# Seven block products for five units a layer, the column units one stage later, and a new order in two later stages

## The chip, the core and the metric

The kernel runs on one NeuronCore of a Trainium2 chip. The metric is the device time of one execution in microseconds (us), the median of several runs. TensorE is called PE here, VectorE DVE, ScalarE ACT, GpSimd POOL, and SyncE, which only issues transfers, SP.

## The reference

The input is one sequence of 256 tokens by 1024 features, in float32. It passes through two blocks; each has two layers.

```python
def first_block(x, ...):
    for l in range(2):
        u = rms_norm(x, pre_norm_g[l]) @ w_in[l]        # 1024 -> latent, sb, moba, conv, gate columns
        o_a = mla_attention(...)                         # from 352 latent columns and two up matrices
        o_b = stick_breaking_attention(q_b, k_b, v_b)    # 4 heads of 64
        o_c = moba_attention(q_c, k_c, v_c, rel_bias)    # 4 heads of 64, biased by distance
        o_d = conformer_conv(u_conv, ...)                # 31 taps, layer norm, 256x256
        y = concat(o_a, o_b, o_c, o_d) * silu(u_gate)    # 1024 gate columns
        x = x + rms_norm(y @ w_out[l], post_norm_g[l])

def second_block(x, c, w_ada, ...):
    for i in range(2):
        sh1, sc1, g1, sh2, sc2, g2 = split(silu(c) @ w_ada[i] + b_ada[i], 6)
        u = x * (1 + sc1) + sh1
        y = gla_mixer(u) if i == 0 else chunk_attention(u)     # 16 heads of 64 in the attention
        x = layer_norm(alpha * x + (1 + g1) * y)
        u = x * (1 + sc2) + sh2
        y = square(relu(u @ ff_w1[i])) @ ff_w2[i]              # 1024 -> 4096 -> 1024
        x = layer_norm(alpha * x + (1 + g2) * y)
```

The row c has 1024 features and is the same for all tokens, so silu(c) @ w_ada is a product of a vector and a matrix: 2 layers of 1024x6144.

## The kernel before

The stages follow each other on one core: first block, layer 0 and layer 1; the input product of the GLA mixer, its chunks and its output; feed-forward 0; the attention in four groups of four heads ("qd" 0 to 3 in the code); feed-forward 1. Each engine has one program of its own, written out by hand, and waits on semaphores; nothing is planned at run time. An instruction never passes another on the same engine, so the order of the calls in each engine's block is the order of the work.

**Weights.** All large weights are cut into units of 128x2048 float32 (1 MB). They lie in one array in the order of use, and SP (L483) copies unit n into slot n modulo 6 of the tile `raw` as soon as unit n-6 has been used. SP issues strictly in order: unit n+1 isn't issued before unit n. The orders are strings: in the first block, "w" is a weight unit and "a" a column unit; in the mixer "m" and "a"; in a feed-forward "u" (up), "d" (down) and "a".

**Column units.** The 48 units of w_ada are multiplied by the row silu(c) on DVE: column_unit (L982) runs two multiply-and-reduce instructions over 128x1024 for one unit, which then frees its slot. Before, 12 of them stand in each layer of the first block, 11 in the GLA mixer and 13 in feed-forward 0. `coefficients(s)` (L1062 and on, a few small instructions) turns their sums into the scale and shift of stage s.

**A layer of the first block.** unit_t (L1971) multiplies one unit by the transposed tokens hT: 16 matmuls of 128 weight columns by 256 tokens, which the profile counts as 32 (a float32 matmul has two records), and which give 256 columns of the product. Ten units go through it in a layer: U_CA, U_CG, U_BQ, U_BK, U_CQ, U_CK and four gate units; the value units have a form of their own (L1981), the latent units go through first_units (L2024). The order on PE is: latent products; conv, stick-breaking and moba units; the scores; for each pair of heads a gate unit, the transposes of the probabilities (turn, L1998), the product with the values (L2164), and in between the conv's transposes (L2219, which need cnat from DVE L1315) and its 256x256 product (L2234, into a bank that gate 3 has to be read out of first); then the output product in seven block products (L2040). On DVE the order is: norms, column units, the conv's 31 taps, the stick-breaking sums (L1232 to L1244), then per pair: gate (L1256), two score maxima (head_max, L1046 and L1049), their reciprocals (L1056), one column unit; after the second pair the conv's mean and variance (L1305), inv_root (L964 to L973) and cnat.

**Seven block products.** For output products, GLA inputs, feed-forwards and attention projections the kernel already uses a scheme of Strassen's kind: a 2x2 block product by seven block products in place of eight, with sums of weight blocks and of token blocks before and sums of products after. The sums are on DVE (mixer_weights L1725 to L1730, mixer_sums L1738 and on, up_sums L1590 to L1595), in the attention on POOL (quad_weights L578 to L583, four instructions for one unit) and DVE (quad_sums L1864 to L1873).

**The attention.** Its 16 units are W0 to W15, in that order with nothing between. For qd = 0, 1, 2 POOL runs quad_weights(3*qd+3), then head_biases(qd+1) (L593 to L596: the value bias and the table of distances of the next four heads), then quad_weights of the two units after it; quad_weights(u) works on the unit W(3+u). DVE runs two maxima, quad_sums(3*qd), two maxima, the next queries (L1885), reciprocals 2 and 3 (L1056), quad_sums(3*qd+1), in the first two groups two pieces of the residual (L1544), quad_sums(3*qd+2), the group's output (L1943) and the next group's value rows (L1894, which wait for head_biases). PE runs the seven products of the units (quad_unit, L2625) between the scores, the turns and the products with the values.

**Feed-forward.** In a group g, PE runs half of the up products of group g+1 (L2342), the first half of the down products of group g (L2315), the rest of the up products, and the second half of the down products.

```python
with sp.Fori(1, N_UNITS // SLOTS) as i:                                         # L480
    for s in range(SLOTS):
        sp.wait_ge(used[s], i)
        sp.dma_start(raw[:, s, :], units[i * SLOTS + s, :, :]).then_inc(landed[s], 16)
```

Of the kernel before, what the change touches and what calls it, by code (L numbers as in the profile page):

```python
# [11 lines left out]
ALU = mybir.AluOpType  # L12
ACT = mybir.ActivationFunctionType
# [24 lines left out]
A1 = 12  # L38
# [5 lines left out]
ORDER = "wwwawwawwawawawa" "wawawawa" "wwawwa"  # L44
# [5 lines left out]
U_GATE = (U_G0, U_G1, U_G2, U_G3)  # L50

# [30 lines left out]
GLA_ORDER = 4 * "mma" + "mmaaaa" + "mmmmmmaaa"  # L82
FF_ORDER = ("u" + 13 * "uda" + "ud" + "dud", "u" + 14 * "ud" + "dud")
# [3 lines left out]
N_FF1 = N_ATT + 16  # L87
# [10 lines left out]
AG = len(GA_AT)  # L98

ADA_1 = [N_GLA + n for n in GA_AT] + places(FF_ORDER[0], "a", N_FF0)  # L100
assert len(GW_AT) == 16 and len(ADA_1) == 24
# [34 lines left out]
def build(nc, x, units, cols, small, post_g, consts, onehot, rel_bias, crow_in, colb_in,  # L136
          ln_rows, low_in, gk_in, att_line, v_row, out):
    with ExitStack() as ctx:  # L138
# [13 lines left out]
        HB = ((G[2], G[3]), (G[0], G[1]))  # L152
# [114 lines left out]
        early = sb("early", [P, 4, P])  # L267
# [52 lines left out]
        ones_ready, rr_psum, rr_ready = sem("ones_ready"), sem("rr_psum"), sem("rr_ready")  # L320
# [17 lines left out]
        qk_ready = event("qk_ready", 4)  # L338
# [23 lines left out]

        fixed_ready = sem("fixed_ready")
        colb_ready, gla_in, lnrow_in, line2_in = (sem(n) for n in ("colb_ready", "gla_in", "lnrow_in", "line2_in"))
        gcol_ready, gate_out, row_in = sem("gcol_ready"), sem("gate_out"), [sem(f"row_in{g}") for g in range(2 * DEPTH)]
        tb_ready = sem("tb_ready")
# [68 lines left out]
        OUT_UNITS.append(tuple(N_ATT + 12 + w for w in range(4)))  # L435
# [7 lines left out]
        OUT_W.append([[ada[:], xs[:, 1, :], row(tline), crow[:]],  # L443
# [8 lines left out]
        out_block = [gateT[:].rearrange("p a b -> p (a b)")[:, 512 * i:512 * (i + 1)] for i in range(4)]  # L452

# [36 lines left out]
        def _(pool):  # L490
# [5 lines left out]
            pool.memset(relb[:], 1.0).then_inc(ones_ready, 1)  # L496
# [24 lines left out]
            pool.wait_ge(ones_ready, 1)  # L521
# [26 lines left out]
            store_gate(0)  # L548
            for l in range(1, DEPTH):
                layer_vectors(l)  # L550
            store_gate(1)

            pool.wait_ge(x_new.sem, 2 * DEPTH + 2)
            for g in range(2):
                load_gate(g)
# [7 lines left out]

            norm_rows(1)
# [4 lines left out]
            def quad_weights(u):  # L569

                n = N_ATT + 3 + u
# [4 lines left out]
                if u >= 3:  # L576
                    wait_used(pool, 0, n - 3)
# [13 lines left out]
            def head_biases(qd):  # L591
                pool.wait_ge(line2_in, 16 * (qd + 2))
                pool.tensor_copy(vcur[:], vrow[:, GW * qd:GW * (qd + 1)]).then_inc(cur_ready.sem, 1)  # L593
                pool.tensor_copy(tcur[:], tline[:, :, ::-1]).then_inc(tb_ready, 1)
                pool.wait_ge(tb_ready, qd + 1)
# [9 lines left out]

            store_gate(3)
            load_gate(3)
# [17 lines left out]
            norm_rows(2)  # L625
            norm_rows(3)

        @block.scalar
        def _(act):
# [79 lines left out]
            for l in range(DEPTH):  # L709
# [54 lines left out]
                wait_used(act, T1 * l, U_CQ)  # L764
                act.activation(qkC[:, 0], G[0][:], ACT.Copy, scale=HD_SCALE).then_inc(qk_ready.sem, 1)
                wait_used(act, T1 * l, U_CK)
                act.activation(qkC[:, 1], G[1][:], ACT.Copy).then_inc(qk_ready.sem, 1)
# [7 lines left out]

                def gate_tanhs(g):
                    wait_used(act, T1 * l, U_GATE[g])
                    if g >= 1:
                        act.wait_ge(silu_ready.sem, silu_ready.at(l, g))
                    act.activation(th[:].rearrange("p c s -> p (c s)"), G[1][:], ACT.Tanh, scale=0.5).then_inc(gate_tanh.sem, 1)  # L780
# [7 lines left out]
                for g in range(H):  # L788
                    gate_tanhs(g)
                    for j in (2 * g, 2 * g + 1):  # L790
                        head_copy(8 * l, j, (A[3], A[0]))
                    if g < H - 1:
# [118 lines left out]
            def keys(qd):  # L911
                act.wait_ge(bc_ready.sem, bc_ready.at(qd, 1))
                if qd == 0:
                    wait_used(act, 0, N_ATT + 1)
# [42 lines left out]
        def _(dve):  # L957
# [31 lines left out]
            def gate_columns(g, n):  # L989

                wait_used(dve, 0, n)
                dve.wait_ge(colb_ready, 16)
                dve.scalar_tensor_tensor(gcol[:, g, :], gacc[:, g, :], 1.0, colb[:, B_GATE + KC * g:B_GATE + KC * (g + 1)],
                                         ALU.add, ALU.add).then_inc(gcol_ready, 1)
# [1903 lines left out]
```

## Time and profile before

| | us |
|---|---|
| median of 3 runs (lowest, highest) | 976.6 (975.53, 977.18) |
| the profiled execution, whole | 975.87 |
| its span, first to last instruction | 974.0 |
| PE busy | 957.1 |
| DVE busy | 758.5 |
| ACT busy | 230.7 |
| POOL busy | 83.7 |

| stage, us from the span's start | PE busy | DVE busy | POOL busy | DMA share |
|---|---|---|---|---|
| layer 0, 0 to 155.4 | 153.5 | 110.5 | 11.5 | 0.68 |
| layer 1, 155.4 to 304 | 146.8 | 111.7 | 4.3 | 0.58 |
| GLA mixer, 304 to 432 | 127.6 | 115.2 | 2.5 | 0.61 |
| feed-forward 0, 432 to 640 | 206.0 | 187.3 | 7.9 | 0.71 |
| attention, 640 to 760 | 119.9 | 73.6 | 56.9 | 0.44 |
| feed-forward 1 and the end, 760 to 974 | 203.3 | 160.2 | 0.5 | 0.39 |

A row of the timeline gives the start, the time to the end, the engine, the line, the operation with its output and input, the shape (partitions on both sides for a matmul, then partitions by columns) and the number of like instructions merged. In square brackets stands the idle time just before it and what ended it; a row without brackets started with no idle time worth showing. The end of a matmul is modelled and overlaps the next one, so the pitch of matmuls is read from start to start.

### The profile page before, as it was taken

How to read it: one execution, taken by the hardware profiler on the slowest of the kernel's cores; microseconds unless marked ns; L12 is line 12 of the kernel's file. 1: busy time of each engine (PE TensorE's matmuls, PEld its weight loads, DVE VectorE, ACT ScalarE, POOL GpSimd, SP SyncE). 2: the span in 40 equal slices, each digit the busy share in tenths (PEclk: the TensorE clock that was granted, in tenths of full speed). 3: DMA queues.
4: the chain of work that ended last, by engine and by line, in shares of the span. 5: the costliest groups of instructions: out<-in, count | busy, mean ns of one | idle time of the engine just before them, and what ended most of it. 6: DMA issues, size and time to landing. Idle time of an engine off the chain costs nothing. (4 is left out here: it accounts for less than half of the span.)

```text
span 974.0 us, 14339 instructions
## 1 busy us (share of the span) xinstructions
PE 957.1 (98%) x5354; PEld 711.0 (73%) x5354; DVE 758.5 (78%) x1719; ACT 230.7 (24%) x580; POOL 83.7 (9%) x100
## 2 busy tenths in 40 slices
PE   9999999999999999999999999999999999999996
PEld 5858855858857998757777777689994767777764
DVE  2796687696688898999999888955667877766687
ACT  4134425125433222111000000123333200000002
POOL 2100000000001000000001000056830000000000
PEclk9999999999999999999999999999999999999999
DMA  9954653855555766574779777535444254544411
GB/s 354 379 201 191 234 201 149 350 197 226 196 215 209 288 220 257 178 297 149 245 289 336 284 257 259 189 131 195 152 173 147 103 184 173 216 173 174 173 44 44
DMA packets 31069, 205.38 MB, mean 211 GB/s; under 512 B 3640, under 2 KB 4845, under 8 KB 7709
## 3 DMA queue, kind: packets, MB, share of 16 engines
q1 hardware_dynamic: 27740, 190.94, 52.9%
q0 software_dynamic: 3264, 13.57, 3.9%
q8 instruction: 43, 0.70, 0.3%
q14 instruction: 22, 0.17, 0.1%
HBM read 203.42 MB, written 1.07 MB: 210 GB/s over the span
## 5 line engine op out<-in xcount | busy, mean ns | idle before, releaser
L1971 PE MATMUL bank<-hT,raw 128*128 128x256 f32 x736 | 162.5, 380 | 0.0
L1971 PEld LDWEIGHTS bank<-hT,raw 128*128 128x128 f32 x736 | 138.9, 190 | 21.2 <-issue 2.4
L982 DVE CUSTOM_DVE_ANT_0 raw<-raw,crow 128x1024 f32<-128x1024 f32 x96 | 113.2, 1222 | 6.7 <-DMA raw<-units_dram 5.3
L2315 PE MATMUL bank<-yT,arena 128*128 128x512 f32 x224 | 100.8, 593 | 0.1
L2315 PE MATMUL bank<-raw,arena 128*128 128x512 f32 x180 | 86.8, 593 | 0.0
L2315 PEld LDWEIGHTS bank<-yT,arena 128*128 128x128 f32 x224 | 42.5, 190 | 54.0 <-issue 51.9
L2342 PEld LDWEIGHTS bank<-hT,raw 128*128 128x128 f32 x416 | 50.4, 192 | 11.5 <-issue 11.5
L839 ACT ACTIVATE arena<-bank 128x512 f32<-128x512 f32 x26 | 15.6, 598 | 179.3 <-PE bank L2342 179.3
L2342 PE MATMUL bank<-hT,raw 128*128 128x128 f32 x416 | 50.6, 275 | 0.0
L1024 DVE SCALAR_TENSOR_TENSOR arena<-arena 128x256 f32<-128x256 f32 x120 | 49.2, 485 | 0.1
L2342 PE MATMUL bank<-arena 128*128 128x128 f32 x336 | 42.2, 275 | 3.0 <-issue 3.0
L2342 PEld LDWEIGHTS bank<-arena 128*128 128x128 f32 x336 | 39.8, 192 | 4.6 <-issue 4.6
L2342 PE MATMUL bank<-arena,gateT 128*128 128x128 f32 x336 | 42.1, 275 | 0.0
L2315 PEld LDWEIGHTS bank<-raw,arena 128*128 128x128 f32 x180 | 29.9, 191 | 16.3 <-issue 16.3
L2342 PEld LDWEIGHTS bank<-arena,gateT 128*128 128x128 f32 x336 | 39.8, 192 | 0.0
L2040 PE MATMUL bank<-arena 128*128 128x512 f32 x88 | 39.7, 592 | 0.0
L2342 PEld LDWEIGHTS bank<-arena,raw 128*128 128x128 f32 x224 | 29.4, 192 | 13.4 <-issue 13.4
L841 ACT ACTIVATE arena<-bank 128x384 f32<-128x384 f32 x28 | 13.8, 492 | 106.8 <-PE bank L2342 106.8
L2286 PE MATMUL bank<-hT,raw 128*128 128x128 f32 x244 | 37.4, 283 | 1.3 <-ACT hT L700 1.1
L2286 PEld LDWEIGHTS bank<-hT,raw 128*128 128x128 f32 x244 | 33.0, 191 | 4.3 <-issue 3.0
L1602 DVE TENSOR_TENSOR arena<-arena 128x256 f32<-128x256 f32 x26 | 11.4, 440 | 31.0 <-ACT arena L839 30.8
L2040 PEld LDWEIGHTS bank<-arena 128*128 128x128 f32 x88 | 16.6, 190 | 19.8 <-issue 19.7
(471 smaller groups left out, 1767.9 us busy)
## 6 DMA issues: line engine op xcount, KB each, us to landing
raw<-units_dram SPq DMA_DIRECT2D x178, 1024.0 KB, 4.9
arena<-ln_rows_dram POOLq DMA_DIRECT2D x4, 1024.0 KB, 5.0
arena<-gate_scratch POOLq DMA_DIRECT2D x4, 512.0 KB, 5.5
arena<-att_line_dram POOLq DMA_DIRECT2D x4, 512.0 KB, 5.8
arena<-small_dram POOLq DMA_DIRECT2D x2, 896.0 KB, 10.5
raw<-units_dram SPq DMA_DIRECT2D x2, 704.0 KB, 7.5
xt<-x_dram SPq DMA_DIRECT2D x2, 512.0 KB, 5.4
arena<-post_g_dram POOLq DMA_DIRECT2D x2, 512.0 KB, 8.4
```

What stands on the lines that cost most here:

```text
L839: act.activation(prod[:, 0:4].rearrange("p i n -> p (i n)"), A[0][:], ACT.Copy).then_inc(prod_ready.sem, 1)
L841: act.activation(prod[:, 4:7].rearrange("p i n -> p (i n)"), A[0][:, 0:3 * P], ACT.Copy).then_inc(prod_ready.sem, 1)
L982: ins = dve.tensor_tensor_reduce(out=w, in0=w, in1=crow[:], scale=1.0, scalar=0.0, op0=ALU.mult, op1=ALU.add, accum_out=dst[:, c:c + 1])
L1024: ins = dve.scalar_tensor_tensor(cacc[:, c, :], xg[:, c, j:j + S], w, cacc[:, c, :], ALU.mult, ALU.add)
L1602: ch.do(dve.tensor_tensor(csum[:, 0:5:4], p[:, 0:1].to_broadcast([P, 2, P]), p[:, 1:3], ALU.add))
L1971: mm = pe.matmul(b[:, c * S:(c + 1) * S], raw[:, s, k * 256 + c * P:k * 256 + (c + 1) * P], act_t[:, k, :], start=(k == 0), stop=(k == KC ...
L2040: mm = pe.matmul(OUT_BANKS[l][j][:], x[c] if isinstance(x, list) else x[:, c], y[c] if isinstance(y, list) else y[:, 512 * c:512 * (c + 1) ...
L2286: mm = pe.matmul(b[:, c * S + t * P:c * S + (t + 1) * P], raw[:, n % SLOTS, k * 256 + c * P:k * 256 + (c + 1) * P], hT[:, k, t * P:(t + 1) ...
L2315: mm = pe.matmul(SB[i][:], x, y, start=g == 0, stop=stop)
L2342: mm = pe.matmul(b[:, i * P:(i + 1) * P], x(k), y(k), start=k == 0, stop=k == 3)
```

## The change

Five units of each layer of the first block, U_CQ, U_CK and gates 1 to 3, are multiplied by seven block products: first_tokens makes four sums of token blocks once a layer, first_weights four instructions of 128x512 for a unit (one writes into the unit itself), first_seven 28 matmuls of 128 columns by 128 tokens (56 records in the profile), ACT two copies out of the banks, first_outputs six instructions of 128x128 and 128x256. Gates 1 to 3 are read from the tile `early` in place of a bank. Gate(g) now stands on DVE after first_outputs, the two maxima and the reciprocals of its pair; before, it stood ahead of them.

The 48 column units keep their number and their own cost, but 6 stand in each layer of the first block, 12 in the mixer, 12 in feed-forward 0, 8 in the attention and 4 in feed-forward 1. coefficients(1) stands in the middle of the mixer in place of its start.

In both feed-forwards the products of group 1 get another order; POOL's loading of two gate rows is moved; at the seam of the layers ACT does the second layer's first tile in two halves; in the GLA input the second tile's transposes come two steps earlier.

```diff
-ORDER = "wwwawwawwawawawa" "wawawawa" "wwawwa"
+ORDER = "wwwawwa" "wwwawwa" "wwawwa" "wwww"
-GLA_ORDER = 4 * "mma" + "mmaaaa" + "mmmmmmaaa"
-FF_ORDER = ("u" + 13 * "uda" + "ud" + "dud", "u" + 14 * "ud" + "dud")
+GLA_ORDER = 4 * "mma" + "mmaaaa" + "mmmmmmaaaa"
+ATT_ORDER = "www" "aa" "wwwa" "aa" "wwwa" "aa" "wwwwwww"
+FF_ORDER = ("u" + 2 * "ud" + "aua" + 10 * "dua" + "du" + "ddud",
+            "u" + 2 * "ud" + "aua" + 2 * "dua" + 9 * "du" + "ddud")
+ATT_UNITS = ((0, 1), (2, 3, 4), (5, 6, 7), ())
@@ ACT, first block
+                for i, (u, b) in enumerate(((U_CQ, G[0]), (U_CK, A[2]))):
+                    act.activation(first_prod[i][:, 0:4]..., b[:], ACT.Copy, scale=scale)
+                    wait_used(act, T1 * l, u)
+                    act.activation(first_prod[i][:, 4:7]..., G[1][:, 0:3 * P], ACT.Copy, scale=scale)
@@ ACT, seam of the layers
                     y_square(l, 1, 0)
+                    layer_input(l + 1, 0, 0, KC // 2)
                     y_square(l, 1, 1)
-                    layer_input(l + 1, 0, 0, KC)
+                    layer_input(l + 1, 0, KC // 2, KC)
@@ DVE, first block
+            def first_tokens(l):
+                ch.do(dve.tensor_tensor(first_tsum[:, 0], b[0][1], b[0][0], ALU.subtract))
+                ch.do(dve.tensor_tensor(first_tsum[:, 2], b[1][1], b[0][1], ALU.subtract))
+                ch.do(dve.tensor_tensor(first_tsum[:, 1], b[1][1], first_tsum[:, 0], ALU.subtract))
+                dve.tensor_tensor(first_tsum[:, 3], b[1][0], first_tsum[:, 1], ALU.subtract)
+            def first_weights(l, i):
+                wait_landed(dve, T1 * l, U_SEVEN[i])
+                ch.do(dve.tensor_tensor(d[1], a[0][0], a[1][0], ALU.subtract))
+                ch.do(dve.tensor_tensor(a[1][0], a[1][0], a[1][1], ALU.add))
+                ch.do(dve.tensor_tensor(d[0], a[1][0], a[0][0], ALU.subtract))
+                dve.tensor_tensor(d[2], a[0][1], d[0], ALU.subtract)
+            def first_outputs(l, i, o):
+                dve.wait_ge(fprod_ready.sem, fprod_ready.at(l, 2 * i + 2))
+                ch.do(dve.tensor_tensor(c[:, 0], p[:, 0], p[:, 2], ALU.add))
+                ch.do(dve.tensor_tensor(o[:, 0], p[:, 0], p[:, 1], ALU.add))
+                ch.do(dve.tensor_tensor(c[:, 1], c[:, 0], p[:, 3], ALU.add))
+                ch.do(dve.tensor_tensor(c[:, 2], c[:, 0], p[:, 5], ALU.add))
+                ch.do(dve.tensor_tensor(o[:, 2:4], c[:, 1:2]..., p[:, 4:6], ALU.add))
+                ch.do(dve.tensor_tensor(o[:, 1], c[:, 2], p[:, 6], ALU.add))
+                first_tokens(l)
                 if l == 0:
                     silu_row()
-                    ada_unit(l, 0)
-                ada_unit(l, 1)
+                    ada_unit(0)
+                ada_unit(A1 * l + 1)
...
-                ada_unit(l, 2)
+                ada_unit(A1 * l + 2)
                 taps(0, 12)
-                ada_unit(l, 3)
                 taps(12, 20)
...
+                first_weights(l, 0)
+                first_weights(l, 1)
                 taps(20, TAPS)
-                ada_unit(l, 4)
...
-                ada_unit(l, 5)
-                ada_unit(l, 6)
+                first_outputs(l, 0, qkC[:, 0]...)
+                ada_unit(A1 * l + 3)
...
+                first_outputs(l, 1, qkC[:, 1]...)
+                first_weights(l, 2)                        # ahead of the loop over the heads
                 for j in range(2 * H):
                     if j % 2 == 0:
-                        gate(j // 2)
+                        if j == 0:
+                            gate(0)
+                        else:
+                            first_outputs(l, 1 + j // 2, early)
...
-                        if j < 6:
-                            ada_unit(l, 7 + j // 2)
+                        if j > 0:
+                            gate(j // 2)
+                        if j == 2:
+                            first_weights(l, 4)
+                        if j < 4:
+                            ada_unit(A1 * l + 4 + j // 2)
+                        if j == 0:
+                            first_weights(l, 3)
@@ DVE, end of a layer
-                ada_unit(l, 10)
@@ DVE, mixer
-            coefficients(1)                                # at its start
             for a in (6, 7):
-                ada_unit_1(ADA_1[a], a)
+                ada_unit(GA + a)
+            coefficients(1)
-            for a in (8, 9, 10):
-                ada_unit_1(ADA_1[a], a)
+            for a in (8, 9, 10, 11):
+                ada_unit(GA + a)
             mixer_output(MIXER, MIX_S, OUT_BANKS[MIXER])
@@ DVE, attention
                 head_inverse(h0, 2)
                 head_inverse(h0, 3)
+                for a in ATT_UNITS[qd]:
+                    ada_unit(AH + a)
+                    if a == 2 * H - 1:
+                        coefficients(3)
@@ PE, first block
-                unit_t(T1 * l, U_CQ, hT, G[0])
-                unit_t(T1 * l, U_CK, hT, G[1])
+                first_seven(l, 0, G[0], G[1])
+                pe.wait_ge(upc_ready.sem, upc_ready.at(l, 6))
+                first_seven(l, 1, A[2], G[1])
...
-                    unit_t(T1 * l, U_GATE[g], hT, G[1])
+                        pe.wait_ge(pt_ready.sem, 8 * l + 2 * g)
+                        first_seven(l, g + 1, G[1], A[0])  # for g of 1 to 3
@@ PE, feed-forward
+                    if g == 1:
+                        seven_products(s, down[g], g, 0)
                     if g > 0:
                         up_products(s, n, g + 1, "half")
-                    seven_products(s, down[g], g, 0)
+                    if g == 1:
+                        seven_products(s, down[g], g, 1, stage="input")
+                    else:
+                        seven_products(s, down[g], g, 0)
                     up_products(s, n, g + 1, "rest")
-                    seven_products(s, down[g], g, 1)
+                    seven_products(s, down[g], g, 1, stage="weights" if g == 1 else None)
@@ PE, input of the GLA mixer
                 for k in range(KC):
+                    if t == 0 and k == KC - 2:
+                        input_transposes(1)
                     mm = unit_columns(n, G[1], t, 1)(k)
-                if t == 0:
-                    input_transposes(1)
```

## Rows read from the trace of the kernel before

**Rows 1.** Page, part 1: engine, busy us, share of span, instructions.

```profile
PE 957.1 (98%) x5354; PEld 711.0 (73%) x5354; DVE 758.5 (78%) x1719; ACT 230.7 (24%) x580; POOL 83.7 (9%) x100
```

**Rows 2.** Timeline of PE, first block: start us, us, engine, line, operation.

```profile
20.80 20.99 PE L1971 MATMUL bank<-hT,raw 128*128 128x256 f32 x96
...
82.74 1.97 PE L2132 MATMUL bank<-kst,arena 128*96 128x128 f32 x16
...
98.62 7.07 PE L1971 MATMUL bank<-hT,raw 128*128 128x256 f32 x32
...
118.00 0.60 PE L2219 MATMUL bank<-kst,arena 128*128 128x128 f32 x4
...
132.99 1.32 PE L2234 MATMUL bank<-arena 128*128 128x256 f32 x5
...
158.09 4.97 PE L2024 MATMUL bank<-raw,hT 128*128 128x352 f32 x16 [1.32 <-ACT hT L685]
```

**Rows 3.** Timeline of DVE, first block, first layer.

```profile
41.13 1.23 DVE L982 CUSTOM_DVE_ANT_0 raw<-raw,crow 128x1024 f32<-128x1024 f32 x1 [2.21 <-DMA raw<-units_dram]
...
78.82 1.36 DVE L1238 TENSOR_TENSOR arena<-arena,kst 128x256 f32<-128x256 f32 x3
...
98.34 0.29 DVE L1046 CUSTOM_DVE_ANT_0 probs<-bank,kst 128x128 f32<-128x128 f32 x1 [0.55 <-PE bank L1990]
...
112.39 1.23 DVE L982 CUSTOM_DVE_ANT_0 raw<-raw,crow 128x1024 f32<-128x1024 f32 x1
...
114.69 0.16 DVE L964 TENSOR_SCALAR guess<-ms 128x2 int32<-128x2 int32 x1
...
116.85 1.00 DVE L1315 TENSOR_SCALAR arena<-bank,bag,rs 128x256 f32<-128x256 f32 x2
```

**Rows 4.** Timeline of DVE at 318 us: four sums of one unit, then the next.

```profile
318.78 0.69 DVE L1725 TENSOR_TENSOR arena<-raw 128x512 f32<-128x512 f32 x1
...
321.31 0.69 DVE L1725 TENSOR_TENSOR gateT<-raw 128x512 f32<-128x512 f32 x1
```

**Rows 5.** Timeline of PE around the GLA mixer and in the first feed-forward.

```profile
313.01 0.46 PE L2286 MATMUL bank<-hT,raw 128*128 128x128 f32 x2 [0.37 <-ACT hT L700]
...
431.01 1.06 PE L2057 MATMUL bank<-kst,xs 128*128 128x128 f32 x8
...
457.61 2.02 PE L2342 MATMUL bank<-arena 128*128 128x128 f32 x16 [1.51 <-issue]
```

**Rows 6.** Timeline of DVE at the end of the GLA mixer.

```profile
430.12 0.81 DVE L1419 TENSOR_SCALAR xs<-xt,bag,rst 128x1024 f32<-128x1024 f32 x1
```

**Rows 7.** Timeline of SP's DMA queue in the attention.

```profile
649.75 0.33 SPq L483 DMA_DIRECT2D raw<-units_dram  x1
```

**Rows 8.** Page, part 6: output, input, queue, KB each, us from issue to landing.

```profile
raw<-units_dram SPq DMA_DIRECT2D x178, 1024.0 KB, 4.9
```

**Rows 9.** Timeline of POOL in the attention.

```profile
667.40 1.28 POOL L578 TENSOR_TENSOR arena<-raw 128x512 f32<-128x512 f32 x1 [5.49 <-PE bank L2625]
...
673.94 0.30 POOL L596 MEMSET arena<- 64x256 f32 x1
...
678.62 2.26 POOL L581 TENSOR_TENSOR gateT<-gateT,raw 128x512 f32<-128x512 f32 x1
```

**Rows 10.** Timeline of DVE in the attention.

```profile
672.56 0.21 DVE L1056 RECIPROCAL rinv<-rsum 128x2 f32<-128x2 f32 x2
...
676.12 0.29 DVE L1864 COPY arena<-bank 128x128 f32<-128x128 f32 x1 [3.34 <-PE bank L2625]
...
678.13 3.83 DVE L1544 TENSOR_TENSOR xt<-xs,arena 128x1024 f32<-128x1024 f32 x2 [0.22 <-DVE arena L1873]
...
687.25 0.28 DVE L1046 CUSTOM_DVE_ANT_0 probs<-bank,arena 128x128 f32<-128x128 f32 x1
```

**Rows 11.** Timeline of PE in the attention.

```profile
686.39 1.95 PE L2625 MATMUL bank<-arena 128*128 128x128 f32 x16
...
690.86 0.91 PE L1998 MATMUL bank<-kst,probs 128*128 128x128 f32 x6
```

More of the change, by code:

```diff
@@ L1677, in tile_residual, with side_unit @@
                 ch.sync()
+            def side_unit(lay, g):
+                if g < (AH - AF0, len(ADA_AT) - AF1)[lay]:
+                    ada_unit((AF0, AF1)[lay] + g)
+                    if lay == 0 and g == 2 * H - 1:
+                        coefficients(2)
             def groups(s):
@@ L1694, in groups @@
                     up_half_sums(s, g + 1)
-                    weight_sums(down[g])
+                    if g == 1:
+                        side_unit(lay, 0)
+                    else:
+                        weight_sums(down[g])
                     up_rest_sums(s, g + 1)
@@ L1701, in groups @@
                         weight_sums(down[SEVEN - 1], wsum_last)
+                    if g == 0:
+                        wait_used(dve, 0, down[0])
+                        weight_sums(down[1])
                     if 1 <= g <= 4:
                         x_piece(s - 1, g - 1)
-                    if lay == 0 and AG + g < len(ADA_1):
-                        ada_unit_1(ADA_1[AG + g], AG + g)
-                        if AG + g == len(ADA_1) - 1:
-                            coefficients(2)
-                            coefficients(3)
+                    if g > 0:
+                        side_unit(lay, g)
                 dve.wait_ge(row_in[s], 16)
@@ L2072, in _ @@
                     first_units(l, t)
+                    if l > 0 and t == 0:
+                        first_columns(T1 * l, U_CA, G[0], t)
                 if l == 0:
@@ L2076, in _ @@
                     pe.matmul(A[3][0:H, 0:384], relb[:], oneh[:], start=True, stop=True).then_inc(rr_psum, 1)
-                unit_t(T1 * l, U_CA, hT, G[0])
+                if l > 0:
+                    first_columns(T1 * l, U_CA, G[0], 1)
+                else:
+                    unit_t(T1 * l, U_CA, hT, G[0])
                 unit_t(T1 * l, U_CG, hT, G[1])
@@ L2306, in unit_columns, with seven_products @@
                 return column
-            def seven_products(s, n, g, part=None, stop=False, wsum=wsum):
+            def seven_products(s, n, g, part=None, stop=False, wsum=wsum, stage=None):
                 k = g % 3
@@ L2324, in seven_products @@
                     product(1, a[0][1], b[1][0])
-                if part != 0:
+                if part != 0 and stage != "weights":
                     pe.wait_ge(hsum_ready.sem, hsum_ready.at(s // 2, g + 1))
                     product(2, hsum[:, k, 3], b[1][1])
+                if part != 0 and stage != "input":
                     pe.wait_ge(wsum_ready.sem, wsum_ready.at(s // 2, g + 1))
@@ L2815, in lay_out @@
     cols, small = [], []
+    ada = []
+    for g in range(2 * DEPTH):
+        w, p = i["w_ada_2"][g // 2], 3 * (g % 2)
+        ada += [ada_columns(w, p + a // 4, a % 4) if a < 8 else ada_gate(w, p + 2, a - 8) for a in range(A2)]
     for l in range(DEPTH):
@@ L2827, in lay_out @@
         for a, n in enumerate(A_AT):
-            w = i["w_ada_2"][0]
-            layer[n] = ada_gate(w, 3 * l + 2, a) if a < 4 else ada_columns(w, 3 * l + (a - 4) // 4, a % 4)
+            layer[n] = ada[A1 * l + a]
         units += layer
@@ L2859, in lay_out @@
             w, wo = i["att_w_in_2"][0], i["att_w_out_2"][0]
-            for qd in range(H):
-                units += [t_unit(w, part * D + GW * qd) for part in range(3)]
-            units += [n_unit(wo, 512 * c, half) for half in range(2) for c in range(2)]
+            ws = [t_unit(w, part * D + GW * qd) for qd in range(H) for part in range(3)]
+            ws += [n_unit(wo, 512 * c, half) for half in range(2) for c in range(2)]
+            rest = {"w": iter(ws), "a": iter(ada[AH:])}
+            units += [next(rest[c]) for c in ATT_ORDER]
     b_ada, b_in = i["b_ada_2"].reshape(DEPTH, 6, D), i["att_b_in_2"][0].reshape(3, D)
```

264 lines of the change are left out of this document (178 added, 86 removed).

## The prediction

> **What bounds the kernel now.** I read the page first: PE is busy for 957.1 of 974.0 us, DVE for 758.5, POOL for 83.7 [rows 1]. So PE is the bound, there are 17 us of gaps to win, and else only what PE no longer has to do. But DVE at 78% has little room where it feeds PE, and POOL's small share says nothing of when its results are needed. So I went stage by stage through PE's timeline and asked, at each place where it doesn't wait, how long what it needs had been ready. The reader is to see in the first block rows of PE without a bracket (no wait at the conv's transposes, at its product, at the third gate unit) and one gap of 1.32 at the seam of the layers [rows 2]; gaps of 0.37 and 1.51 further on [rows 5]; in the attention a PE that runs through [rows 11] while SP and POOL work far ahead of it [rows 7, 9].
>
> **First block, PE.** Three units of 256-wide matmuls take 20.99 us with a tail of 0.17, 6.94 a unit [rows 2]. Forty matmuls of 128 by 128 stand between the two rows of PE in the attention, 4.47 us, 0.1118 each [rows 11]; 56 make 6.26. The scheme saves 0.68 a unit, 3.4 a layer, 6.8 in both.
>
> **First block, DVE.** Four sums of a unit take 2.53 from start to start [rows 4]; first_weights has two more waits on its own results, so 2.5 to 2.8, taken 2.7; first_tokens 2.5. quad_sums is six such instructions and a copy in 2.01 [rows 10]; without the copy (0.33) first_outputs is 1.65. A column unit is 2.30 [rows 3]. Per layer: 5 x 2.7 + 2.5 + 5 x 1.65 - 6 x 2.30 = +10.5. In the mean it fits (110 of 155 us busy), and the question is where it falls.
>
> (a) The first layer's third column unit already waits 2.21 for its transfer [rows 3], and stands one place later in the order (behind the second value unit): landing about 2.65 later. From there to the masks of L1238 DVE loses two column units (-4.6) and gets two first_weights (+5.4 to 5.5): it ends some 3.5 late, at 80.1 + 3.5 = 83.6 [rows 3]. PE needs the masks half way through the transposes at 82.74, 83.6 less the 1.4 saved on two units = 82.2 [rows 2]. Wait 1.4, in layer 0 alone; in layer 1 the transfer isn't late.
>
> (b) The conv's transposes (118.00) now start 0.15 after the end of what they need, cnat, whose first half is done at 117.3 and second at 117.85 [rows 2, 3]. From the maximum at 98.34 DVE has, in the new order: two maxima and reciprocals with ACT's exponentials 2.7; column unit 2.3; first_weights 2.7; batch statistics 1.4; first_outputs 1.65; two maxima 1.2; reciprocals with their waits 1.6; gate 0.6; first_weights 2.7; column unit 2.3; inv_root 2.16 (114.69 to 116.85); cnat 1.0 [rows 3]. That is 22.3, so 120.7 by the old clock, against 118.0 - 1.4 = 116.6 on PE, which is spared 0.7 at each of two gates. Wait 4.1 if nothing in between comes late, 4.6 taken; bounds 2 and 6. It occurs in both layers.
>
> (c) gate(3) has to be read out before the conv's product at 132.99 [rows 2], which follows the end of the fourth gate unit (126.3) by 6.7. Behind that unit now stand an ACT copy 0.6, first_outputs 1.65, the output's inputs 1.5 and weights 1.25 (each two to three instructions of the pitch of [rows 4]), a tanh 0.6 and the gate 1.1: 6.7, and five hand-overs of 0.2 to 0.3. Wait 1.5 (0 to 3), in both layers.
>
> At the seam ACT's first half no longer has the y_square before it: 1.3 of the 1.32 gap goes [rows 2]; U_CA in two halves costs 0.2 there. Layer 0: -3.4 + 1.4 + 4.6 + 1.5 = +4.1; layer 1: -3.4 + 4.6 + 1.5 - 1.3 + 0.2 = +1.6. Some of (c) is absorbed in (b): I take **+5.0** for both, bounds -5 and +9.
>
> **GLA mixer.** The second tile's transposes come earlier and the 0.37 gap goes [rows 5]: **-0.4**. At the end DVE hands over the normalised first tile at 430.93 [rows 6] and PE starts its transposes at 431.01 without a wait [rows 5]: no slack, and one column unit more (2.3) stands ahead of that, and coefficients(1) (a few instructions of 0.2) in the middle. **+2.6**, bounds 0 and +3.5.
>
> **Feed-forwards.** The gap of 1.51 ahead of L2342 at 457.61 [rows 5] is PE waiting for the weight sums of the next up unit; feed-forward 1 has a second gap of the same length (two in all, one row stands). The first down products now fill it. After them PE may wait some 0.3 for ACT: **-1.2 each, -2.4**, bounds -3 and +1. Twelve column units for thirteen and four for none leave DVE room.
>
> **Attention: the cost.** Eight column units come into the ring of six slots, whose order is www aa www a aa www a aa wwwwwww. SP is strictly in order, so a weight unit behind two column units isn't issued before the slots ahead of those are free. W6 was issued at 649.75 [rows 7]; an issue takes 4.9 to land [rows 8]. POOL made its sums from 667.40 and was through head_biases(1) at 674.24 [rows 9]; PE asked for the sums only at 686.39 [rows 11], DVE used the table at 687.25 [rows 10]. A lead of 14 and of 13 us.
>
> Now: column units 0 and 1 run on DVE after the reciprocals of 672.56 [rows 10], used at about 675 and 677 (I reckoned 674.4 and 676.7). They hold the slots of column units 3 and 4, which stand ahead of W6 in SP's queue. So W6 is issued at 677.2, with the other two still in transit (2.7 apart): landed 684.8. POOL, which waits for it with head_biases queued behind, is done with the sums (four of 1.27) at 690.2 and with the biases at 692.0. PE does the unit's first two products at 685.1 and waits 0.8 before and 3.4 after; the value rows and the maxima come 5.5 late (692.8 for 687.25), the exponentials and probabilities follow, and the turns, without a wait at 690.86 [rows 11], wait 1.8 more. **+6.0** up to there.
>
> In the next group three column units (6.9) stand before quad_sums(4), by which PE's unit 5 waits 2.4. W9 again waits for two column units: issued 710.4, landed 718.4; waits 2.6 + 3.4 + 1.8. **+10.2**. In the third, column units 5 to 7 and coefficients(3) before quad_sums(7): **+5.8**; the last group's output weights come 0.4 later. Sum **+22.4**.
>
> In that are 5.0 for DVE and POOL against each other: two pieces of the residual take 3.83 next to POOL instructions of 2.26, which are 1.28 elsewhere [rows 9, 10]; column units have the same two inputs in SBUF. The Trainium skill ("SBUF — State Buffer", "Who interferes with whom") says that such a DVE instruction and a GpSimd one that reads SBUF share a port exclusively, and that the other fully blocks. The trace agrees in size: both were stretched by about one length of the other. By that rule the sum stays 22.4, without it 17.4.
>
> **Sum.** 5.0 - 0.4 + 2.6 - 2.4 + 22.4 = +27.2. On the profiled execution (974.0 span and 1.87 around it, 975.87) 1003.1; the median is 0.7 above the profiled one, so 1003.8, and since some waits overlap I predict **1003**. About 0.2%, 2 us, is what a measurement of this kernel can tell from no change.
>
> **Rivals.**
> 1. The ring's delay is mostly covered. For it: leads of 13 and 14 us [rows 9 to 11]. Against it: a delay of 17.7 at POOL's start (667.4 to 685.1) is more than both. If only DVE's added work counted (8 x 2.3, of which DVE's idle time before quad_sums, 3.34 at 676.12 [rows 10], takes a good part), attention +5 to +9: 978 + 7 + 4.8 - 5, near 987.
> 2. Faster: DVE's new work hides everywhere as PE sees it. Then PE keeps -6.8, -1.3, -0.4, -2.4 to -3 and the attention nothing: 975.9 - 11 = 965. It decides at (b), (c) and W6: DVE would have to reach cnat within 18 us, and POOL's sums within the lead of 14. For it: DVE is idle for 22% of the span. Against: each of the three sums above, made from rows, comes out beyond the lead.
> 3. Heavier: the column units' slots also delay W12 to W15 or DVE's waits in the first block add to (a) to (c) in full (+9), and the attention +26: 1011.
> 4. The attention as forecast, but the first block's waits are hidden (-5 for both layers): 993.
>
> **How the numbers follow.** Forecast, attention +17 to +25 and the first block +1 to +8, 0.58; rival 4 0.12; rival 1 0.14; heavier 0.08; faster 0.06; no change 0.02. Range: 985 to 1010 leaves out rival 2, no change and the tail of the heavier case. Faster 0.06, within 0.2% 0.02, slower 0.92.
>
> **What would show it.** In the profile after: PE idle in the attention before the unit of W6 and within it, released by the DMA and by POOL, 3 to 4 us, and again with W9; turns behind them with 1 to 2; SP's issue of W6 near 677 of the old clock; POOL idle for over 20 us before its fourth unit. In the first block PE idle before L2219 of before, 4 to 5 in each layer, released by DVE's cnat. If these waits are there and the total isn't, the feed-forwards hold the error. The prediction is wrong if PE's attention stage grows by less than 12 us, or PE waits for cnat less than 2.

## The result, and the profile after

| | before | after |
|---|---|---|
| median, us (lowest, highest; 4 runs each) | 976.74 (975.53, 977.18) | 1016.35 (1014.49, 1017.27) |
| span of the profiled execution | 974.0 | 1015.1 |
| PE busy | 957.1 | 964.6 |
| DVE busy | 758.5 | 806.5 |
| mean granted clock | 0.998 | 0.979 |

The changed kernel is slower: the ratio is 1.0406, 95% interval [1.0392, 1.0421]. The direction and the places were forecast, the size was not: 1016.35 us against 1003, +39.6 against a sum of +27.2, and a range that ended at 1010.

Part 1 of the page of the changed kernel, against [rows 1]:

```profile
PE 964.6 (95%) x5626; PEld 725.1 (71%) x5626; DVE 806.5 (79%) x1827; ACT 238.5 (23%) x596; POOL 79.7 (8%) x100
```

PE should be busy 6.8 us less and is busy 7.5 more. That is the first sign that its work itself ran slower. The rest is idle time: 1015.1 - 964.6 = 50.5 for 16.9 before, +33.6. So the span's +41.1 is -6.8 of products, +33.6 of waits and a rest of +14.3, which is put down to work at a lower clock (estimate: it is what is left if the products saved what was forecast; where the clock is full their pitch fits, sixteen of them take 1.79 us from 127.72 to 129.51, 0.112 each). The forecast had -6.8, +34.0 and nothing for the third term.

PE's timeline after. The first three rows are layer 0 of the first block, the fourth is the seam of the layers, the last is the first work of feed-forward 0, which waits for the end of the GLA mixer; they answer to [rows 2] and [rows 5]:

```profile
83.76 1.08 PE L2283 MATMUL bank<-kst,arena 128*96 128x128 f32 x8 [1.18 <-DVE arena L1323]
...
120.88 1.11 PE L2377 MATMUL bank<-kst,arena 128*128 128x128 f32 x4 [3.90 <-DVE arena L1411]
...
138.41 1.97 PE L2392 MATMUL bank<-arena 128*128 128x256 f32 x8 [0.54 <-ACT arena L846]
...
162.30 4.97 PE L2119 MATMUL bank<-raw,hT 128*128 128x352 f32 x16
...
442.73 1.09 PE L2201 MATMUL bank<-kst,xs 128*128 128x128 f32 x8 [4.04 <-DVE xs L1500]
```

Waits (a), (b) and (c) are there, with 1.18, 3.90 and 0.54; layer 1 has 4.11 and 0.54. The gap at the seam is gone. The four transposes at 120.88 take 1.11 us, which took 0.60 at 118.00 [rows 2].

Three slices of 5 us of layer 0 after: span, busy time of PE, PEld, DVE, ACT, POOL, then the granted clock, DMA share and GB/s:

```profile
115.00:120.00 5.00, 1.98 (x18) 1.30 (x16) 4.62 (x17) 1.47 (x3) 0.00 (x0) 0.97 0.60 210
120.00:125.00 5.00, 4.12 (x19) 3.14 (x20) 4.65 (x18) 1.17 (x4) 0.00 (x0) 0.50 0.00 0
125.00:130.00 5.00, 5.00 (x40) 5.00 (x40) 3.74 (x6) 3.20 (x11) 0.00 (x0) 0.85 0.00 0
```

A clock of 0.50 is the lower of its two levels, 1.2 GHz. It falls at about 119.7 (the first slice still has 0.97), within the 3.90 in which PE waits from 116.98 on, and is back at about 126.5. The kernel before has no slice under 0.96 before its last matmul; in this one there are seven such stretches, each at a wait of PE or right behind it.

PE's timeline after in the attention:

```profile
696.18 2.05 PE L2789 MATMUL bank<-hT,raw 128*128 128x128 f32 x16 [0.49 <-DMA raw<-units_dram]
701.40 2.02 PE L2789 MATMUL bank<-arena 128*128 128x128 f32 x16 [3.18 <-POOL arena L608]
...
712.31 1.60 PE L2093 MATMUL bank<-kst,probs 128*128 128x128 f32 x6 [6.21 <-ACT probs L668]
...
734.63 3.42 PE L2789 MATMUL bank<-hT,raw 128*128 128x128 f32 x16 [2.59 <-DMA raw<-units_dram]
739.85 2.02 PE L2789 MATMUL bank<-arena 128*128 128x128 f32 x16 [1.80 <-POOL arena L608]
...
750.75 1.60 PE L2093 MATMUL bank<-kst,probs 128*128 128x128 f32 x6 [6.19 <-ACT probs L668]
...
768.04 1.91 PE L2789 MATMUL bank<-raw,arena 128*128 128x128 f32 x8 [2.29 <-DVEq L1966]
```

Here the sixteen matmuls that take 2.05 at 696.18 take 3.42 at 734.63, behind a wait of 2.59. W6 and W9 came late and POOL's sums with them, as forecast (the stage starts 11.4 later than before, so the 696.20 below is 684.8 by the old clock, the forecast's own figure); but the turns (L2093) wait 6.2 each, where 1.8 was forecast. The cause stands in the rows of POOL and DVE after, which answer to [rows 9, 10]:

```profile
696.20 1.27 POOL L603 TENSOR_TENSOR arena<-raw 128x512 f32<-128x512 f32 x1 [18.37 <-DMA raw<-units_dram]
...
702.64 0.30 POOL L621 MEMSET arena<- 64x256 f32 x1
...
703.70 1.29 POOL L603 TENSOR_TENSOR gateT<-raw 128x512 f32<-128x512 f32 x1
...
707.50 1.34 POOL L608 TENSOR_TENSOR gateT<-raw,gateT 128x512 f32<-128x512 f32 x1
```

```profile
702.98 6.14 DVE L1985 TENSOR_TENSOR arena<-arena 128x256 f32<-128x256 f32 x2 [6.28 <-POOL arena L621]
...
709.04 0.28 DVE L1131 CUSTOM_DVE_ANT_0 probs<-bank,arena 128x128 f32<-128x128 f32 x1
```

Two small additions on DVE (the value rows), released at 702.98, end at 709.1: as POOL's memset freed them, POOL also began the four sums of the next unit, and DVE's next instruction starts only at 709.04, when these four have ended. r2_pool_late tests whether the one holds up the other.

Where the time went, by the start of the transposes that open each stage (PE's timeline, both kernels): first block +7.9, GLA mixer +3.8, feed-forward 0 -0.3, attention +30.6, feed-forward 1 -0.9.

### The profile page after: what moved, and what is told of

Same layout as the page of the kernel before. It is cut to its first block and busy times, and to the rows that moved or that the text cites. A ratio compares the mean times of both kernels' runs of the same rounds, so it can differ in the third digit from the quotient of the medians.

```text
span 1015.1 us, 15054 instructions
## 1 busy us (share of the span) xinstructions
PE 964.6 (95%) x5626; PEld 725.1 (71%) x5626; DVE 806.5 (79%) x1827; ACT 238.5 (23%) x596; POOL 79.7 (8%) x100
## 5 line engine op out<-in xcount | busy, mean ns | idle before, releaser
L2066 PE MATMUL bank<-hT,raw 128*128 128x256 f32 x384 | 84.6, 380 | 0.0
L2066 PEld LDWEIGHTS bank<-hT,raw 128*128 128x128 f32 x384 | 72.4, 190 | 10.6 <-issue 1.0
L2501 PEld LDWEIGHTS bank<-hT,raw 128*128 128x128 f32 x416 | 50.4, 192 | 11.5 <-issue 11.5
L2501 PEld LDWEIGHTS bank<-arena 128*128 128x128 f32 x336 | 39.8, 192 | 1.2 <-issue 1.2
L2444 PEld LDWEIGHTS bank<-hT,raw 128*128 128x128 f32 x244 | 33.3, 195 | 3.7 <-issue 2.6
L552 POOL DMA_DIRECT2D gate_scratch<-gcol x4 | 2.2, 554 | 382.7 <-DVE gcol L1046 382.7
```

Of the source, the lines that this page charges most:

```text
L2066: mm = pe.matmul(b[:, c * S:(c + 1) * S], raw[:, s, k * 256 + c * P:k * 256 + (c + 1) * P], act_t[:, k, :], start=(k == 0), stop=(k == KC ...
L2444: mm = pe.matmul(b[:, c * S + t * P:c * S + (t + 1) * P], raw[:, n % SLOTS, k * 256 + c * P:k * 256 + (c + 1) * P], hT[:, k, t * P:(t + 1) ...
L2501: mm = pe.matmul(b[:, i * P:(i + 1) * P], x(k), y(k), start=k == 0, stop=k == 3)
```

## Experiments

Each was timed beside the kernel before on the same chip (976.2 to 976.8).

**r1_ring: the order of the attention's units.**

```diff
-ATT_ORDER = "www" "aa" "wwwa" "aa" "wwwa" "aa" "wwwwwww"
+ATT_ORDER = "wwwwwww" "aa" "www" "aaa" "ww" "aaa" "wwww"
```

> The changed kernel with one line other: the attention's units stand in the array as seven weight units, two column units, three weight, three column, two weight, three column, four weight, so that W6 and W9 are no longer queued behind column units whose slots wait for DVE. DVE's column units stay where they are. Theory A (SP's strict order delays W6 and W9, POOL and the value rows behind them follow, and TensorE's clock falls after the waits): the attention stage, now +30.6 us against the kernel before, keeps only DVE's own delay of quad_sums(4) and (7), +6 to +10; total 1016.4 - 21 = about 995. Rival B (it is the 18 us of added DVE work in the stage that costs, wherever the units lie): the stage stays at +20 or more and the total at 1006 or more.

997.1 (994.9 to 999.9), ratio 1.0221 [1.0195, 1.0247]: 19 us under the changed kernel, and the attention is at +10.4 (781.18 - 645.59 = 135.59 from its first transposes to the next ones, 125.16 before). Same DVE work, no late units: theory A. POOL makes the sums of W6 as soon as PE has freed what they need, and the longest wait left in the attention is the one for quad_sums(7), 4.73, which the prediction had at 5.8; the one for quad_sums(4), forecast at 2.4, is 0.51. POOL's and PE's timelines:

```profile
676.89 1.27 POOL L603 TENSOR_TENSOR arena<-raw 128x512 f32<-128x512 f32 x1 [5.49 <-PE bank L2789]
```

```profile
702.91 1.24 PE L2093 MATMUL bank<-kst,probs 128*128 128x128 f32 x6 [1.24 <-ACT probs L668]
...
746.27 2.02 PE L2789 MATMUL bank<-raw,arena 128*128 128x128 f32 x8 [4.73 <-DVEq L1966]
```

**r2_pool_late: POOL waits before the second unit of a group.**

```diff
                 if qd < H - 2:
+                    pool.wait_ge(nm_ready.sem, HE + H * (qd + 1) + 1)
                     quad_weights(3 * qd + 4)
```

> The changed kernel, with POOL waiting for the next group's first maximum before it starts quad_weights(3*qd+4). Theory A (the value rows, 6.14 us for two instructions that take 0.7 alone, are shut out by POOL's four instructions that start beside them): they take under 1.5 us, the turns behind them wait 1 to 2 us and not 6.2, the granted clock doesn't fall there, and the total drops by 4.7 x 2 for the wait and 1 to 2 x 2 for the clock, to about 1004. Rival B (the turns wait because W6 and W9 land late and the biases with them): a change under 2 us, 1015 to 1017.

1011.9 (1011.2 to 1012.6), ratio 1.0366 [1.0349, 1.0384]: 4.4 under the changed kernel, not 13 and not nothing. The mechanism was right and its worth was not. DVE, then PE:

```profile
701.79 0.76 DVE L1986 TENSOR_TENSOR arena<-arena 128x256 f32<-128x256 f32 x2 [5.67 <-POOL arena L621]
...
713.47 0.62 DVE L1977 TENSOR_SCALAR arena<-arena 128x256 f32<-128x256 f32 x2 [4.22 <-POOL arena L614]
```

```profile
705.75 1.24 PE L2094 MATMUL bank<-kst,probs 128*128 128x128 f32 x6 [0.83 <-ACT probs L669]
...
722.90 2.08 PE L2790 MATMUL bank<-raw,arena 128*128 128x128 f32 x8 [3.04 <-DVEq L1967]
...
761.37 2.08 PE L2790 MATMUL bank<-raw,arena 128*128 128x128 f32 x8 [5.43 <-DVEq L1967]
```

The additions take 0.76 and the turns wait 0.83 and 0.61, 11 us less. But now PE waits for quad_sums(4) and (7), 3.04 and 5.43 where it was 0 and 2.29. These are not DVE's column units alone. DVE's next queries (L1977) need a small copy that POOL makes only behind the eight sums of two units (L614), and they wait 4.22 for it here, and 3.20 in the next group; the column units and quad_sums stand behind them. In the changed kernel they did not wait for it, because DVE itself was late. So POOL's late sums hold DVE at one place or at the other. And the clock falls behind these waits as it did behind the others. Not run: this edit with POOL's copy ahead of the sums.

**r3_cnat_first: the conv's rows first.** In both layers inv_root and cnat stand ahead of first_weights(4) and the column unit.

```diff
                         if j == 2:
+                            inv_root(2 * l + 2, 2)
+                            ... cnat ...                   # taken from j == 3
                             first_weights(l, 4)
```

> The changed kernel, with inv_root and the conv's normalised rows (cnat) on DVE ahead of first_weights(4) and the column unit, in both layers. Theory A (DVE's queue makes PE wait 3.9 and 4.1 us before the conv's transposes, and the granted clock falls to its lower level because of that wait, for another 2.6 us a layer): the wait is under 0.5, no slice of the first block has a clock under 0.95, and the total drops by 6.6 x 2 less 1 to 2 for the sums of gate 3 that now come later, to 1004 or 1005. Rival B (the clock falls for the new form of matmuls, 128 by 128 in place of 128 by 256, and not for the wait): the drop is 4.0 x 2 less 1 to 2, to 1009 or 1010, and the clock still falls. Rival C (the delay only moves to the gate's unit): under 3 us.

1016.8 (1015.3 to 1019.0), ratio 1.0409 [1.0391, 1.0426]: nothing gained, rival C. The wait for cnat is gone, and the same length stands before the conv's product, behind gate(3), in both layers:

```profile
136.05 3.78 PE L2391 MATMUL bank<-arena 128*128 128x256 f32 x8 [4.30 <-DVE gateT L1346]
```

Its eight matmuls take 3.78 here and 1.97 in the changed kernel: the clock falls there too. DVE was late as a whole; the order only chose which of its results PE met first.

**r4_delay: only a wait.** The kernel before, and idle multiplies on DVE ahead of inv_root of the conv.

```diff
                     if j == 3:
+                        for _ in range(2 + 2 * l):
+                            ch.do(dve.tensor_tensor(dly[:], crow[:], crow[:], ALU.mult))
+                            ch.sync()
                         inv_root(2 * l + 2, 2)
```

> The kernel before, with idle work added on DVE ahead of inv_root of the conv: two multiplies of 128x1024 (about 2.5 us) in layer 0 and four (about 5.0) in layer 1; their result is not used. The slack there is 0.15. Theory A (a wait of PE lets the granted clock fall): PE waits about 2.3 and 4.8 us, the clock falls at least after the second, and the total rises by 7.1 and a further 2 to 5, to 986 to 989. Rival B (the clock doesn't depend on such a wait): +7.1, 984, and a clock of 1.00 in all slices. Rival C (DVE catches up elsewhere): under +5.

988.4 (987.9 to 989.3), ratio 1.0126 [1.0109, 1.0143]: theory A. PE's two waits, two slices around the second (columns as above) and part 1 of the page:

```profile
120.70 1.11 PE L2222 MATMUL bank<-kst,arena 128*128 128x128 f32 x4 [2.28 <-DVE arena L1318]
...
275.39 1.12 PE L2222 MATMUL bank<-kst,arena 128*128 128x128 f32 x4 [4.79 <-DVE arena L1318]
```

```profile
270.00:275.00 5.00, 0.61 (x6) 0.37 (x4) 4.55 (x15) 0.87 (x2) 0.00 (x0) 0.92 0.95 356
275.00:280.00 5.00, 4.61 (x17) 3.27 (x18) 3.33 (x13) 1.02 (x5) 0.00 (x0) 0.50 0.16 66
```

```profile
PE 960.8 (97%) x5354; PEld 714.0 (72%) x5354; DVE 766.8 (78%) x1725; ACT 230.5 (23%) x580; POOL 83.4 (8%) x100
```

The program of PE is unchanged (x5354), so the slower work can be read from start to start. From the conv's transposes to the product behind the next gate unit the kernel before takes 8.49 us in both layers (118.00 to 126.49, 266.17 to 274.66); here it takes 10.07 (120.70 to 130.77) and 11.22 (275.39 to 286.61). Two waits, 7.1 us together, brought 1.6 and 2.7 of slower work, 4.3 together; the span grew by 12.2. (PE's busy time rose by 3.7 only, because its matmuls on zeros at the start of the program took 5.21 here and 6.55 before.) So the fall doesn't need the new form of matmuls.

**r6_no_seven: the reordered ring, without the first block's seven products.** first_tokens, first_weights, first_outputs and the copies are out, unit_t is back.

> The run with the reordered ring of the attention (997.1), with the five units a layer multiplied by plain products again, without first_tokens, first_weights and first_outputs; the column units stay one stage later. Theory A (DVE's added sums cause all the waits of the first block, 5.5 us a layer, and the fall of the clock in it): the block is at the old one's length less the 1.3 of the seam, 9 us under the changed kernel's +7.9, and the total 988; what is left over the kernel before is the GLA mixer's end (+3.8) and the attention (+8 to +10). Rival B (the later column units or their landings cause them, as at the masks in layer 0): waits of over 1 us stay in front of the conv's transposes, total over 992.

988.7 (987.9 to 989.2), ratio 1.0127 [1.0111, 1.0142]: theory A. Behind the first 10 us no wait over 0.3 is left in the first block, which is 1.0 shorter than before and 7.4 shorter than in r1_ring: that is what the seven products cost where they stand, after all that they save. What is left is the mixer's end, with the clock fallen (the transposes take 1.97 for 1.06), and the attention, +10.3:

```profile
433.77 1.97 PE L2164 MATMUL bank<-kst,xs 128*128 128x128 f32 x8 [4.01 <-DVE xs L1463]
```

**r5_small: the three small parts alone**, on the kernel before.

> The kernel before with three parts of the change alone: ACT's two halves at the seam of the layers, the second tile's transposes two steps earlier in the GLA input, and the new order of group 1 in both feed-forwards (with column units at the same stages as before, 13 of them in feed-forward 0). No seven products in the first block. Theory A: each fills a gap of PE: 1.3 at the seam, 0.4 at the GLA input, 0.9 in each feed-forward (1.51 less the 0.58 that shows later in the changed kernel); together -3.5, 973.2. Rival B: the feed-forward's order gives nothing, since its gap comes back whole one product later: -1.7, 975. No clock under 1.00 in either case.

974.7 (973.9 to 976.6), ratio 0.9984 [0.9975, 0.9993]: 1.5 gained, not 3.5, and neither theory. The feed-forward's gap shrank from 1.51 to 0.58 (0.65 in the second), as said. The seam's gap only moved, from before the latent products (1.32) to before the second tile's transposes, which wait for DVE (1.69), and in the profiled execution the clock fell behind it. In r7_two_gates, the next run, the same wait of 1.69 stands at the same place, and the same sixteen matmuls behind it take 4.97 and not 6.66. PE in r5_small, then in r7_two_gates:

```profile
163.84 1.09 PE L2024 MATMUL bank<-kst,xs 128*128 128x128 f32 x8 [1.69 <-DVE xs L1102]
165.04 6.66 PE L2036 MATMUL bank<-raw,hT 128*128 128x352 f32 x16
...
470.99 2.02 PE L2355 MATMUL bank<-arena,gateT 128*128 128x128 f32 x16 [0.58 <-issue]
```

```profile
164.10 4.97 PE L2124 MATMUL bank<-raw,hT 128*128 128x352 f32 x16
```

**r7_two_gates: seven products for gates 1 and 2**, on r5_small, column units where they were before; inv_root and cnat right behind the conv's statistics.

```diff
+U_SEVEN = U_GATE[1:3]
                 head_inverse(8 * l, 1)
+                first_weights(l, 0)
...
                         if j < 6:
                             ada_unit(l, 7 + j // 2)
+                        if j // 2 + 1 < 2:
+                            first_weights(l, j // 2 + 1)
```

> The three small parts on the kernel before, and seven products for gates 1 and 2 alone, with the column units where they were (12 a layer) and the conv's normalised rows right behind its statistics, ahead of the second gate. DVE gets 2.5 + 2 x (2.8 + 1.65) = 11.4 us more a layer, into its idle time of 4.7 early in the layer and 7.1 over the four score pairs. Theory A (only a queue that is full where PE asks costs): PE does 0.69 x 2 less a layer and waits under 0.5, total 973.2 - 2.8 + 0.5 = 971. Rival B (any of these sums on DVE makes PE wait at the gates or the conv's product by more than it saves): 974 or more.

973.1 (972.6 to 973.4), ratio 0.9966 [0.9952, 0.9979]. PE waits 0.21 and 0.52 for the new copies and nowhere for the new sums; DVE is busy 779.0 for 758.5. Theory A in its mechanism; the total is 2 higher than said: 1.5 is what r5_small lacked, and four units (two a layer) saved 1.6 on r5_small and not 2.3.

**r8_three_gates: gate 3 too**, on r7_two_gates (`U_SEVEN = U_GATE[1:4]`).

> As the run with gates 1 and 2, and gate 3 as well by seven products, which puts gate(3) on DVE behind first_outputs, the output's inputs and one part of its weights. Theory A: the third saves another 0.69 a layer, but gate(3) stands in front of the conv's product with less lead, as in the run with cnat first (a wait of 4.3 there); DVE's queue is 5 us shorter here, so the wait is 0 to 2 a layer: 969.5 to 974. Rival B: the wait is over 3 us in each layer, and the clock falls: 980 or more.

990.2 (989.6 to 990.5), ratio 1.0140 [1.0125, 1.0156]: rival B. One unit a layer more, with gate(3) behind its sums on DVE, turns a gain of 3 into a loss of 14; layer 1 waits the same 1.18 and 5.26. PE in layer 0:

```profile
121.76 1.16 PE L2140 MATMUL bank<-hT,arena 128*128 128x128 f32 x8 [1.18 <-DVE arena L1092]
...
139.05 3.78 PE L2374 MATMUL bank<-arena 128*128 128x256 f32 x8 [5.25 <-DVE gateT L1341]
```

**r9_columns and r10_no_seam.** On r7_two_gates, the first tile's share of U_CA ahead of the second tile's transposes in layer 1, as the changed kernel has it; and without the halves at the seam.

```diff
                     first_units(l, t)
+                    if l > 0 and t == 0:
+                        first_columns(T1 * l, U_CA, G[0], t)
```

> The run with gates 1 and 2 by seven products (973.1), and in layer 1 the first tile's share of U_CA (32 matmuls of 128 by 128, 3.6 us) ahead of the second tile's transposes, as the changed kernel has it, with the other two banks for those transposes. Theory A: in that run ACT's two halves only moved the gap of the seam, from 1.32 in front of the latent products to 1.69 in front of the second tile's transposes, which wait for DVE; the 3.6 us of U_CA cover it: -1.7 + 0.2, 971.6. Rival B (DVE's tile comes later too, or the banks make it wait): 973 or more.

> The run with gates 1 and 2 by seven products (973.1), without ACT's two halves at the seam. Theory A: without U_CA's share in between the halves are worth nothing (1.32 of gap in one place or 1.69 in the other): 972.5 to 973.5. Rival B: they are worth the 1.3 that the prediction gave them: 974.4.

r9: 971.3 (970.9 to 971.6), ratio 0.9952 [0.9938, 0.9965], theory A: the second tile's transposes start without a wait. r10: 973.1 (972.6 to 974.1), ratio 0.9968 [0.9956, 0.9980], the same as r7: the halves alone are worth nothing. U_CA's share without the halves was not run. PE in r9, at the seam:

```profile
160.50 3.73 PE L2136 MATMUL bank<-hT,raw 128*128 128x128 f32 x32
164.07 1.04 PE L2112 MATMUL bank<-kst,xs 128*128 128x128 f32 x8
```

r9 is the fastest version here: 5 us under the kernel before, 45 under the changed one.

## Why the prediction was right or wrong

The step that failed is a term that the sum doesn't have: the prediction priced each wait of PE at its own length and put the work behind it at nothing. What the runs show in its place is slower work behind many of the waits: 14.3 us by the estimate above, where the whole miss in the span is 13.9 (+41.1 for +27.2). No rival and no end of the range had it either. r4_delay shows it by itself: 7.1 of waits, 4.3 of slower work, in an unchanged program of PE. The Trainium skill ("TensorE: Matmul & The Clock Gate", "What's actually happening") says that TensorE's clock is gated by how busy the engine has been and falls to 1.2 GHz when it idles; the traces agree, in the 0.50 of the slices above.

The sum of the waits came out, +34.0 forecast and +33.6 measured, but partly by luck: in the attention two errors of opposite sign cancel, as the list shows.

By its steps:
- *Products*, -6.8: the pitch of the new matmuls is as said (0.112), the saving by itself was not measured. r6 and r1 have the same rest; the first block without seven products is 7.4 shorter, so if they save 6.8, waits and clock cost 14 there.
- *(a)* 1.4: 1.18, in layer 0 alone, as said. *(b)* 4.6: 3.90 and 4.11, right, nearer to the sum of the rows (4.1) than to the value taken. *(c)* 1.5: 0.54, too high; but r3 shows that (b) and (c) are one lateness of DVE, 4 to 5 us, met at one place or the other.
- *Seam*, -1.3 + 0.2: the gap is gone, but the prediction gave it to ACT's two halves. r10 shows them worth nothing alone; it takes U_CA between the tiles (r9), which the prediction named only as a cost.
- *GLA mixer*, +2.6: the wait is 4.04. The column unit added was priced by DVE time only (2.3), not by its landing, and it came late: DVE waited 0.99 for it. That is most of the miss; with 11 column units in the mixer (r7, r9) PE waits 0.3 at most there.

```profile
430.09 1.23 DVE L1029 CUSTOM_DVE_ANT_0 raw<-raw,crow 128x1024 f32<-128x1024 f32 x1 [0.99 <-DMA raw<-units_dram]
```

- *Feed-forwards*, -2.4: -1.2 together. The gap gave 0.9 in each, in place of 1.2, and the clock falls at the start of feed-forward 0.
- *Attention*, +22.4: its waits are 22.8, the stage +30.6; the other 7.8 are left for slower work. But the 22.8 are not made as forecast. The late units cost 0.5 + 3.2 and 2.6 + 1.8 (forecast 0.8 + 3.4 and 2.6 + 3.4); the turns 6.2 twice for 1.8 twice, since DVE's additions waited through four POOL instructions and not one; and quad_sums(4) and (7) 0 and 2.3 for 2.4 and 5.8. With no late units (r1) these two are 0.51 and 4.73, so the forecast had them too high; the rest of the difference is argued and not shown: DVE gained on a PE that stood elsewhere. The turns are 8.8 over the forecast, the other waits 8.4 under it.
- *The Trainium skill's rule on the shared port*: it was used with one instruction of each engine in turn. In this trace the second addition of DVE waited through four POOL instructions in a row (6.14 for 0.76), so that the other engine blocks held here for a series. Nor did the price (5.0) apply where the prediction put it: the residual's two pieces took 2.36 after, POOL being idle by then. Where POOL does work beside them, in r1_ring, they take 3.71 and 3.44, and an instruction of a column unit up to 2.27 for 1.22.
- *Rivals*: rival 2 (hidden everywhere) fell, and its condition is what r7 and r9 meet: with two gates DVE's work does hide. Rival 3 (1011) lay nearest, but by luck: PE waits for no landing of W12 to W15, and the first block's waits were no longer than forecast. Rival 1's sum is 984.8 and not 987 as written, and no row shows its 978; r1_ring, which takes the ring's delay away, stands at 997.

Not shown: at which waits exactly the clock falls. It fell at 2.28, 2.29, 2.59, 3.90, 4.04 and 6.2, and not behind 3.18 and 1.80; a wait of 1.69 brought a fall in r5_small and none in r7_two_gates. So the length of the one wait doesn't settle it. It also differs between executions of one kernel: the four of r1_ring took 994.9, 995.1, 999.1 and 999.9 us, with mean granted clocks of 0.991, 0.991, 0.985 and 0.985.

## What to carry to other kernels

Where PE runs without gaps, price each new wait as its length and, as a range, 0 to 3 us more for slower work behind it (2 in the mean of the seven stretches here); the kernel before shows no price for that, so make one wait on purpose and measure it. Before adding work to an engine that is busy for 78%, ask at each place where the bound engine takes its results how early they now are: two units a layer fitted in that lead and a third cost 17 us. And in a ring that is filled strictly in order, place a unit by when the slots of the units queued ahead of it are freed, not by when it is used: the same units in another order were 19 us apart.

## What was not expected of the hardware

- A wait of PE of 2.28 us was followed by matmuls at half speed (four transposes 1.11 for 0.60), one of 3.18 was not (sixteen matmuls 2.02). The same wait of 1.69 was followed by slower matmuls in one run and not in another (6.66 and 4.97).
- Two additions of 128x256 on DVE took 6.14 us next to four POOL additions of 128x512, and 0.76 without them; POOL's were hardly longer (1.29 to 1.45 for 1.27). POOL kept the turn through all four.
